# A two-layer decoder trunk on one core: two thirds of the expert weight matrices by accumulating scatters instead of one-hot products

## The chip, the core and the metric

The kernel runs on one core of one Trainium2 chip. The metric is the device time of one execution in microseconds, and less is better. The engines are named as in the profile: PE (TensorE) multiplies matrices, DVE (VectorE) and ACT (ScalarE) work element by element, POOL (GpSimd) issues here most of the transfers between memory and SBUF, every indirect one among them, and SP issues the weight loads. PEld is PE's loading of the stationary operand, which overlaps its products.

## The reference, cut to what matters

Two layers, each a mixer part and an expert part ("PEER"); the change is about the expert part alone. For 512 tokens and 16384 experts per layer:

```python
def block(xt):                       # 128 tokens of 1024 columns
    q = (xt @ w_pq).reshape(128, 8, 2, 128)
    s = einsum('thpd,hpkd->thpk', q, sub_keys)
    v1, i1 = top_k(s[:, :, 0], 16)   # per head: 16 best of 128 first keys
    v2, i2 = top_k(s[:, :, 1], 16)   # and of 128 second keys
    cand = v1[..., :, None] + v2[..., None, :]
    top, pos = top_k(cand, 16)       # the 16 best pairs of a head
    eidx = i1 * 128 + i2 at pos      # an expert is a pair of keys
    g = softmax(top)
    a = gelu(einsum('thkd,td->thk', u_tab[eidx], xt))
    return einsum('thk,thkd->td', g * a, v_tab[eidx])
```

Each token thus has 8 heads x 16 = 128 chosen experts with a weight each.

## The kernel before

**Two ways through the experts.** The tokens lie in four blocks of 128. Three blocks (`DB = 3`, 384 tokens, `SD`) go the dense way: PE computes the hidden value of every expert for every token, from 128 panels of `u_tab` (128 experts each), ACT applies gelu and writes the 128 x 384 result to memory (`h_d`, "expert_spill" in the trace). The weights of the same tokens stand in a second matrix in memory (`g_d`, "weight_spill"), of which nearly all entries are zero. In the last stage both are read back, multiplied on DVE (`wgt`) and used as stationary operand against 128 panels of `v_tab`. The fourth block goes the sparse way: 128 indirect gathers fetch one chosen row of `u_tab` for each token, 4 KB each (`urow`), and one product and sum on DVE, a "dot", follows for each; later 128 gathers of `v_tab` rows follow the same way (`vrow`).

**A panel** is a 1024 x 128 weight block. SP loads it (`raw`), ACT rounds it (`split_hi`), DVE subtracts the rounded part (`split_lo`, one pass over 128 x 1024), and PE multiplies in three passes of eight (`gemm`, L458 to L460), over 384 columns, or over 512 for the mixer and `w_pq`. ACT and DVE prepare a panel two ahead (`LEAD = 2`); four raw and four split buffers go round.

**Stages of the expert part**, in the order of every engine's program:
1. Heads: eight heads, each with 2 panels of `w_pq` and `T_U = 8` panels of `u_tab`. Beside them DVE finds the best keys and pairs of the head (`best`, `rest`, `pairs`, `pairs_at`, `pairs2`, `places`), and beside the first two panels of the next head it looks up the keys (`key_of`, three passes over 128 x 1024 for each of two sides).
2. R1: `REST = 8` panels. At their start DVE ends the last head, takes the softmax of all heads at once and writes `idu`, the rows to gather, for all 128 slots. POOL waits for that, gathers six rows (`UR = 6` buffers), and after that each row once the dot that frees its buffer is done. After the sixth panel (`SEL_AT`) PE turns the key numbers and weights round, so that the 128 slots of a token stand on the partitions.
3. G: `N_G = 48` groups of `GT = 8` tokens, a panel beside each. DVE compares the key numbers with 0 to 127 (`hot`, two passes over 128 x 1024), ACT scales the first by the weights (`scale_hot`, eight instructions), and PE multiplies the two for each token (L938): that gives the token's 128 x 128 weight matrix. ACT copies it out of PSUM to `stage`, and POOL writes `stage` to `g_d` after each four groups (32 tokens, 2 MB).
4. R2: `REST = 8` panels. V: the 128 panels of `v_tab`, with the last dots and the `v_tab` gathers beside them.

The table `DOTS` says how many dots DVE does after each panel from R1 on (two beside most panels of R1 and R2, three beside two groups of G, then 24 panels of V). Every engine runs its own program in order, so a wait on DVE for a gathered row holds back the next `split_lo`, and with it PE two panels on. POOL's program is one order as well:

```python
pool.wait_ge(idu_ready, l + 1)
for k in range(UR):
    gather_u(k)
for n in range(LATE_U):              # then along R1, G, R2
    for k in range(dots_by(n - 1) if n else 0, dots_by(n)):
        if k + UR < SLOTS:
            gather_u(k + UR)         # waits for dot k
```

Of the kernel before, what the change touches and what calls it, by code (L numbers as in the profile page):

```python
# [15 lines left out]
ACT = mybir.ActivationFunctionType  # L16
# [8 lines left out]
P = 128  # L25
# [12 lines left out]
NEG = -3.0e38  # L38
PH, TOPK, NKEYS = 8, 16, 128
# [6 lines left out]
N_G = SD // GT  # L46
# [14 lines left out]
T_U = 8  # L61
# [8 lines left out]
M_R2 = M_G + NTB * BLK_U  # L70
# [4 lines left out]
A_R2 = A_G + NTB * BLK_U  # L75
# [77 lines left out]
LATE_U = 2 * REST + NTB * BLK_U  # L153
DOTS_V = 24
DOTS = [0, 0] + [2] * (REST - 2) + [1, 2] * (N_G // 2) + [2] * (REST - 2) + [0, 0] + [1, 1, 2] * (DOTS_V // 3)

# [6 lines left out]
def dots_by(p):  # L163

    return sum(DOTS[:p + 1])
# [18 lines left out]
class Chain:  # L184
# [3 lines left out]
    def __init__(self, eng, sem, per_layer):  # L188
        self.eng, self.sem, self.per_layer = eng, sem, per_layer
        self.layer, self.base, self.n = 0, 0, 0  # L190

    def start(self, layer):
        self.layer, self.base, self.n = layer * self.per_layer, 0, 0

    def mark(self, ins):
        ins.then_inc(self.sem, 1)
        self.n += 1

    def wait(self):
        self.eng.wait_ge(self.sem, self.layer + self.base + self.n)  # L200

    def link(self, ins):
        self.mark(ins)
        self.wait()

    def enter(self, i, count):

        self.outer, self.inner, self.count = self.base, self.n, count
        self.base, self.n = i * count + (self.base + self.n), 0

    def leave(self, times):
        assert self.n == self.count, (self.n, self.count)
        self.base, self.n = self.outer, self.inner + times * self.count


DVE_CHAIN = 266


def build_trunk(nc, xT, c, pos, freq, bands, w_mod, b_mod, w_in, w_sT, b_s, qkv_gain, w_uq, w_ukv,
                w_pool, pool_scale, w_abc, w_o, w_pq, keysT, uT_tab, u_rows, v_tab, fin_gain, out, dve_chain):  # L220
# [29 lines left out]
    ones = sb("ones", [P, P])  # L250
    causal = sb("causal", [P, P])
    ident16 = sb("ident16", [P, P], BF16)
    causal16 = sb("causal16", [P, P], BF16)
    iota = sb("iota", [P, P])
    eps = sb("eps", [P, 1])
    cos = sb("cos", [P, TT, HALF])
# [56 lines left out]
    sel1T = sb("sel1T", [P, S])  # L313
    sel2T = sb("sel2T", [P, S])
    gT = sb("gT", [P, SD])
# [84 lines left out]
    g_sub, g_exp, g_norm = sem("g_sub"), sem("g_exp"), sem("g_norm")  # L400
    sel_turned, sel_act, sel_dve = sem("sel_turned"), sem("sel_act"), sem("sel_dve")
# [183 lines left out]
    def _(pool):  # L585
# [19 lines left out]
        pool.wait_ge(consts_made, 2)  # L605
        for half in range(2):
            pool.dma_start(g_d[half, 0:1, 0, :16], ones[0:1, :16]).then_inc(stage_out[half], 16)
        for l in range(DEPTH):
# [10 lines left out]
            pool.dma_start(ukv[:].rearrange("p a b -> p (a b)"), one(w_ukv)).then_inc(params_in, 16)  # L619
            for j in range(3 * KC):  # L620
# [57 lines left out]
            pool.wait_ge(idu_ready, l + 1)  # L678
            for k in range(UR):
                gather_u(k)  # L680
            for n in range(LATE_U):
                for k in range(dots_by(n - 1) if n else 0, dots_by(n)):
                    if k + UR < SLOTS:
                        gather_u(k + UR)
                b = n - REST
                if 0 <= b < NTB * BLK_U and b % BLK_U == BLK_U - 1:
# [4 lines left out]
                    if b == NTB - 1:  # L691
# [3 lines left out]
                r = n - REST - NTB * BLK_U  # L695
# [5 lines left out]
                if r == 1:  # L701
                    pool.wait_ge(stage_out[0], 16 + l * (8 * NTB) + 8 * NTB)
                    pool.wait_ge(stage_out[1], 16 + l * (8 * NTB) + 8 * NTB - 16)
# [5 lines left out]
            pool.wait_ge(stage_out[1], 16 + l * (8 * NTB) + 8 * NTB)  # L709
# [26 lines left out]
    def _(pe):  # L736
        pe.wait_ge(consts_made, 2)
        pe.wait_ge(identr_made, 1)
        with pe.Fori(0, DEPTH) as l:
# [145 lines left out]
            settle(pe)  # L885
            with pe.Fori(0, PH // 2) as two:
# [350 lines left out]
    def _(dve):  # L1237
# [55 lines left out]
        for l in range(DEPTH):  # L1293
# [254 lines left out]
            for h in range(PH):  # L1548
# [232 lines left out]
```

## Time and profile before

| | us |
|---|---|
| median of 3 runs | 3599.91 |
| lowest of them | 3599.59 |
| the profiled execution | 3599.65 |
| its span, first to last instruction | 3597.9 |
| PE busy in the span | 3484.4 (97%) |
| DVE busy | 2483.5 (69%) |
| ACT busy | 1463.0 (41%) |
| POOL busy | 879.9 (24%) |

The first layer's expert part lies from about 447 us to 1790 us after the span's start, the second's about 1775 us later with the same picture. The profile names an instruction by its line in the kernel, its engine, its operation and what it writes and reads, as `urow<-in_u_rows,idu`.

### The profile page before, as it was taken

Reading aid. Unit: us, or ns where it says so; the run is one execution under the profiler, and the core shown is the slowest. Engines: PE = TensorE matmul, PEld = TensorE weight load, DVE = VectorE, ACT = ScalarE, POOL = GpSimd, SP = SyncE. Lnnn points to the kernel's source line nnn. Section 1 sums busy time; section 2 is a strip of 40 time slices with the busy share of each in tenths; the row PEclk is TensorE's granted clock in tenths of the full one; section 3 lists DMA queues with packets and bytes.
Section 4 is the critical chain, followed back from the end, with each engine's and each line's share of the span. In section 5 each row is a group of like instructions: output and inputs, shape, how many; then the busy total and the mean of one; then the engine's idle time right before and its main releaser. Section 6 shows DMA issues by size and latency. Waiting matters only on the chain.

```text
span 3597.9 us, 53854 instructions
## 1 busy us (share of the span) xinstructions
PE 3484.4 (97%) x18220; PEld 2936.6 (82%) x18220; DVE 2483.5 (69%) x4639; ACT 1463.0 (41%) x2538; POOL 879.9 (24%) x1027
## 2 busy tenths in 40 slices
PE   5999999999999999999989998999999999999998
PEld 3776789999999777777767776999999997777775
DVE  6455688889888775555464566888898878655554
ACT  3334233335776333323243333333367753323322
POOL 0010100004334534444400010000053345344442
PEclk8999999999999999999999999999999999999999
DMA  7353434447999988999744433444499999899995
GB/s 258 116 190 125 149 122 148 146 150 287 355 342 340 395 326 338 358 350 346 290 148 153 161 127 120 149 150 150 147 339 345 342 359 379 300 357 352 357 349 199
DMA packets 269525, 909.67 MB, mean 253 GB/s; under 512 B 32212, under 2 KB 65028, under 8 KB 268452
## 3 DMA queue, kind: packets, MB, share of 16 engines
q0 software_dynamic: 126496, 473.44, 35.8%
q1 hardware_dynamic: 105984, 383.83, 29.8%
q10 hardware_dynamic: 36868, 50.35, 3.9%
q8 instruction: 74, 1.21, 0.1%
q14 instruction: 103, 0.84, 0.1%
HBM read 792.14 MB, written 115.34 MB: 252 GB/s over the span
## 4 chain that ended last, share of the span: by engine, by line
PE 92%; DVE 3%; DMA 3%; issue 1%; ACT 1%; POOL 0%; ACTq 0%; SPq 0%; DVEq 0%; POOLq 0%
PE ps L458 16%; PE ps L460 15%; PE ps L459 15%; PE ps L958 10%; PE ps L959 10%; PE ps L960 10%; PE ps L938 5%; PE ps L972 3%; PE ps L776 2%; DMA urow<-in_u_rows,idu 1%; PE ps L832 1%; DMA mod<-in_w_mod 1%; PE ps L899 1%; PE ps L873 1%; PE ps L874 1%
## 5 line engine op out<-in xcount | busy, mean ns | idle before, releaser
L458 PE MATMUL ps<-mov,whl 128*128 128x384 f32 (+1 forms) x2880 | 1042.5, 362 | 48.2 <-DVE whl L445 30.4
L460 PE MATMUL ps<-mov,whl 128*128 128x384 f32 (+1 forms) x2880 | 1014.8, 352 | 0.0
L459 PE MATMUL ps<-mov,whl 128*128 128x384 f32 (+1 forms) x2880 | 1012.2, 351 | 0.0
L445 DVE TENSOR_TENSOR whl<-raw,whl 128x1024 fp32r<-128x1024 f32 x648 | 793.3, 1224 | 205.1 <-ACT whl L435 188.1
L435 ACT CAST whl<-raw 128x1024 fp32r<-128x1024 f32 x648 | 680.0, 1050 | 107.3 <-ACT hst L1148 74.8
L958 PE MATMUL ps<-whl,wgthl 128*128 128x512 f32 x1536 | 614.3, 400 | 14.9 <-DVE wgthl L1646 14.8
L458 PEld LDWEIGHTS ps<-mov,whl 128*128 128x128 f32 x2880 | 543.0, 189 | 102.9 <-issue 38.5
L959 PE MATMUL ps<-whl,wgthl 128*128 128x512 f32 x1536 | 610.6, 398 | 0.0
L960 PE MATMUL ps<-whl,wgthl 128*128 128x512 f32 x1536 | 610.1, 397 | 0.0
L667 POOL DMA_INDIRECT urow<-in_u_rows,idu x256 | 304.5, 1189 | 1225.7 <-DVE idu L1579 787.3
L460 PEld LDWEIGHTS ps<-mov,whl 128*128 128x128 f32 x2880 | 542.3, 188 | 35.3
L459 PEld LDWEIGHTS ps<-mov,whl 128*128 128x128 f32 x2880 | 543.7, 189 | 31.4 <-issue 2.4
L1208 ACT CAST wgthl<-wgt 128x384 fp32r<-128x384 f32 x256 | 131.3, 513 | 830.6 <-PE ps L960 630.4
L1646 DVE TENSOR_TENSOR wgthl<-wgt,wgthl 128x384 fp32r<-128x384 f32 x256 | 142.8, 558 | 379.1 <-ACT wgthl L1208 332.0
L958 PEld LDWEIGHTS ps<-whl,wgthl 128*128 128x128 f32 x1536 | 290.3, 189 | 110.8 <-issue 25.2
L960 PEld LDWEIGHTS ps<-whl,wgthl 128*128 128x128 f32 x1536 | 290.4, 189 | 70.8
L959 PEld LDWEIGHTS ps<-whl,wgthl 128*128 128x128 f32 x1536 | 290.5, 189 | 69.3
L1592 DVE CUSTOM_DVE_ANT_0 urow<-urow,htok 128x1024 f32<-128x1024 f32 x256 | 306.4, 1218 | 35.2 <-DMA urow<-in_u_rows,idu 35.1
L675 POOL DMA_INDIRECT vrow<-in_v_tab,idv x256 | 264.0, 1031 | 259.5 <-PE ps L972 190.7
L1148 ACT ACTIVATE hst<-ps 128x384 f32<-128x384 f32 x256 | 123.5, 483 | 364.9 <-PE ps L460 349.6
L1175 ACT ACTIVATE hotg<-hotg,gT 128x128 f32<-128x128 f32 x768 | 234.9, 391 | 10.7 <-DVE hotg L1601 10.7
L657 POOL DMA_DIRECT2D hin<-expert_spill x256 | 144.6, 570 | 352.4 <-DVE wgt L1634 334.2
(245 smaller groups left out, 3453.9 us busy)
## 6 DMA issues: line engine op xcount, KB each, us to landing
raw<-in_uT_tab SPq DMA_DIRECT2D x256, 512.0 KB
raw<-in_v_tab SPq DMA_DIRECT2D x256, 512.0 KB
expert_spill<-hst ACTq DMA_DIRECT2D x256, 192.0 KB
hin<-expert_spill POOLq DMA_DIRECT2D x256, 192.0 KB
gt<-weight_spill POOLq DMA_DIRECT2D x64, 768.0 KB
weight_spill<-stage POOLq DMA_DIRECT2D x22, 2048.0 KB
raw<-in_w_in SPq DMA_DIRECT2D x72, 512.0 KB
raw<-in_w_mod SPq DMA_DIRECT2D x64, 512.0 KB
```

The source lines that it names most:

```text
L435: nc.scalar.copy(whl[:, m % RING, 0], raw[:, raw_n(m) % RAW]).then_inc(hi_done, 1)
L445: nc.vector.tensor_tensor(whl[:, m % RING, 1], raw[:, raw_n(m) % RAW], whl[:, m % RING, 0].bitcast(F32), ALU.subtract).then_inc(lo_done, 1)
L458: nc.tensor.matmul(o, w[:, 0, k], src[:, 0, k, :cols], start=(k == 0), stop=False)
L459: nc.tensor.matmul(o, w[:, 0, k], src[:, 1, k, :cols], start=False, stop=False)
L460: mm = nc.tensor.matmul(o, w[:, 1, k], src[:, 0, k, :cols], start=False, stop=(k == KC - 1))
L667: pool.indirect_dma_start(urow[:, k % UR], None, u_rows, bass.IndirectOffsetOnAxis(idu[:, k:k + 1], 0)).then_inc(u_in[k % UR], 16)
L675: pool.indirect_dma_start(vrow[:, slot], None, v_tab.rearrange("a p d -> (a p) d"), bass.IndirectOffsetOnAxis(idv[:, q, j:j + 1], 0)).then ...
L958: nc.tensor.matmul(o, ghi, hi, start=first, stop=False)
L959: nc.tensor.matmul(o, ghi, lo, start=False, stop=False)
L960: mm = nc.tensor.matmul(o, glo, hi, start=False, stop=last)
L1175: ins = nc.scalar.activation(one, one, ACT.Copy, scale=gT[:, e * GT + t:e * GT + t + 1])
L1592: nc.vector.tensor_tensor_reduce(urow[:, k % UR], urow[:, k % UR], htok[:], 1.0, 0.0, ALU.mult, ALU.add, act_in[:, k:k + 1]).then_inc(dot_ ...
```

## The change

Of the three dense blocks only the first keeps the one-hot products (`OHB = 1`, `OH = 128` tokens, so `N_G = 16` groups). For the other two (`N_TS = 2`, 256 tokens):
- Their part of `g_d` is filled with zeros at the start of each layer, by eight transfers of 2 MB from a zeroed tile, issued by POOL after the loads of `uq` and `ukv`.
- After each head DVE computes, for the two blocks, at which element of `g_d` each of the 16 weights of a token belongs (`chosen`, table `idg`), and POOL issues 16 x 2 = 32 indirect transfers, each of one 4-byte weight per partition, 128 in all, that add to memory (`scatter`). The 32 of a head wait until all of the head before have landed. That is 256 such transfers in a layer.
- The softmax is taken head by head (`shares`; ACT's Exp stands beside the tenth panel of a head), and the rows to gather are known head by head too. So 8 dots stand beside each head from the second to the eighth (`DOTS_H`), 56 in all, and 72 remain for R1, G, R2 and 18 panels of V. POOL puts the gathers for them behind the 27th to the 32nd scatter of each head, save the last.
- A head has `T_U = 12` panels of `u_tab` instead of 8. With 16 groups instead of 48 the sum stays: 96 + 8 + 16 + 8 = 128 panels.
- PE turns the fourth block's tokens round (`turn_rows`) in the first head and no longer after the last, and 5 tiles instead of 11 after the sixth panel of R1.
- The helper that numbers DVE's chained steps (`Chain`) is shortened to what is used.

```diff
-T_U = 8
+T_U = 12
+N_TS = 2
+OHB = DB - N_TS
+OH = OHB * P
+N_OH = OH // TB
+N_G = OH // GT
+DOTS_H = (0, 0, 0, 0, 0, 0, 0, 0, 0, 1, 1, 2, 2, 2)
+DOTS_A = sum(DOTS_H) * (PH - 1)
+DOTS_V = 18
...
+            for b in range(N_OH, NTB):
+                pool.dma_start(g_d[:, :, b].rearrange("a p x -> p a x"),
+                               zero[:].unsqueeze(1).to_broadcast([P, P // AG, P])).then_inc(zero_out, 16)
...
-            pool.wait_ge(idu_ready, l + 1)
-            for k in range(UR):
-                gather_u(k)
+            def scatter(h):
+                pool.wait_ge(idg_ready, l * PH + h + 1)
+                pool.wait_ge(g_norm, l * PH + h + 1)
+                pool.wait_ge(sc_out, l * (16 * N_TS * SLOTS) + 16 * N_TS * TOPK * h)
+                late = list(range(h * sum(DOTS_H), (h + 1) * sum(DOTS_H))) if h + 1 < PH else []
+                for n in range(N_TS * TOPK):
+                    k, t = h * TOPK + n // N_TS, n % N_TS
+                    settle(pool)
+                    pool.indirect_dma_start(g_d.rearrange("a p b (x o) -> (a p b x) o", o=1),
+                                            bass.IndirectOffsetOnAxis(idg[:, t, k:k + 1], 0),
+                                            topv[:, OHB + t].rearrange("p h k -> p (h k)")[:, k:k + 1], None,
+                                            compute_op=ALU.add).then_inc(sc_out, 16)
+                    if n >= 26 and late:
+                        gather_u(late.pop(0) + UR)
+                for k in late:
+                    gather_u(k + UR)
+            for h in range(PH):
+                pool.wait_ge(idu_ready, l * PH + h + 1)
+                if h == 0:
+                    for k in range(UR):
+                        gather_u(k)
+                scatter(h)
...
+            def shares(h):
+                dve.wait_ge(g_exp, l * PH + h + 1)
+                sums, share = den[:, h * TT:(h + 1) * TT], topv[:, :, h]
+                chain.link(nc.vector.tensor_reduce(sums, share, AX, ALU.add))
+                chain.link(nc.vector.reciprocal(dinv[:, h * TT:(h + 1) * TT], sums))
+                nc.vector.tensor_tensor(share, share, dinv[:, h * TT:(h + 1) * TT].unsqueeze(2).to_broadcast([P, TT, TOPK]),
+                                        ALU.mult).then_inc(g_norm, 1)
+
             for h in range(PH):
                 for j in range(2 + T_U):
                     split_lo(dve, l, M_T + h * (2 + T_U) + j + LEAD)
                     if j < 2 and h:
                         key_of(h - 1, j)
+                    if j == 1 and h:
+                        chosen(h - 1)
+                    if j == 10:
+                        shares(h)
+                    if h:
+                        at = (h - 1) * sum(DOTS_H)
+                        dots_between(at + sum(DOTS_H[:j]), at + sum(DOTS_H[:j + 1]))
```

Two places show it in the programs. **POOL, from the heads to G.** Before, its whole row from the load of the keys to the first write of `stage`:

```order
L648 DMA keys<-in_keysT 128x2048 [waits merged,gemm_done]
L667 DMA urow<-in_u_rows,idu 128x1024 [waits idu_ready,dot_done]
L667 DMA urow<-in_u_rows,idu 128x1024 [waits dot_done] x23
L694 DMA weight_spill<-stage 128x32x128 [waits stage_ready]
```

Now, from the gathers at the end of the seventh head's scatter on (a gather's line is L671 in the new kernel, a scatter's L691):

```order
L671 DMA urow<-in_u_rows,idu 128x1024
L691 DMA weight_spill<-topv,idg 6291456x1
L671 DMA urow<-in_u_rows,idu 128x1024 x3
L691 DMA weight_spill<-topv,idg 6291456x1 x32
L671 DMA urow<-in_u_rows,idu 128x1024 x18
L722 DMA weight_spill<-stage 128x32x128
```

The 32 scatters of the last head stand in one piece, with no gather among them, and the 18 gathers for R1 and the first groups of G stand behind them.

**DVE, at the end of the last head and the start of R1.** Before:

```order
L445 TENSOR_TENSOR whl<-raw,whl 128x1024
L1571 COPY den<-topv 128x32
L1572 TENSOR_TENSOR topv<-topv,den 128x512
L1541 TENSOR_TENSOR eq<-abf,iota 128x1024
...
L1577 SCALAR_TENSOR_TENSOR idf<-sel_106,sel_107 128x128
L1579 TENSOR_SCALAR idu<-idf,lbase 128x128
L445 TENSOR_TENSOR whl<-raw,whl 128x1024
L1582 TENSOR_REDUCE den<-topv 128x32
L1583 RECIPROCAL dinv<-den 128x32
L1584 TENSOR_TENSOR topv<-topv,dinv 128x512
```

Now:

```order
L1620 ISA urow,act_in<-urow,htok 128x1024
L1620 ISA act_in 128x1
L1581 TENSOR_TENSOR eq<-abf,iota 128x1024
...
L1601 SCALAR_TENSOR_TENSOR idf<-sel_108,sel_109 128x16
L1602 SCALAR_TENSOR_TENSOR place<-sel_109,sel_108 128x32
L1603 TENSOR_SCALAR place<-sel_108 128x32
L1604 TENSOR_SCALAR idu<-idf,lbase 128x16
L1605 TENSOR_SCALAR place<-place 128x32
L1606 SCALAR_TENSOR_TENSOR place<-place 128x32
L1611 TENSOR_SCALAR idg<-place,tokat 128x16 x2
```

The dots (`ISA urow,act_in`) stand beside the heads now, the softmax of all heads is gone from here, and behind the last `key_of` come the eight small steps of `chosen` that release the last 32 scatters.

## Rows read from the trace of the kernel before

**Rows 1.** Busy time per engine by stage, first layer: heads, R1, G, R2, V
```profile
core 0: us, PE busy (x) PEld busy (x) DVE busy (x) ACT busy (x) POOL busy (x), PEclk, DMA share, GB/s
...
459.00:831.00 372.00, 370.83 (x2058) 353.85 (x2058) 314.12 (x959) 127.96 (x166) 0.00 (x0) 1.00 0.42 146
831.00:866.00 35.00, 35.00 (x208) 34.97 (x208) 28.61 (x36) 17.29 (x25) 17.25 (x14) 1.00 0.81 306
866.00:1154.00 288.00, 287.89 (x1928) 287.61 (x1927) 253.63 (x298) 224.69 (x528) 106.98 (x87) 1.00 0.98 345
1154.00:1195.00 41.00, 32.70 (x187) 32.07 (x186) 24.65 (x34) 13.05 (x18) 21.71 (x21) 0.96 1.02 385
1195.00:1790.00 595.00, 594.88 (x2772) 445.51 (x2773) 347.03 (x512) 184.96 (x254) 262.38 (x328) 1.00 0.91 345
```
**Rows 2.** Chain that ended last, 840 to 1200 us: start, length, what
```profile
856.32 1.20 PE ps L924 x11
870.01 1.78 PE ps L938 x16
876.09 2.02 PE ps L938 x16
...
1145.13 1.78 PE ps L938 x16
1151.10 1.78 PE ps L938 x16
```
**Rows 3.** ACT's copies of the queries, first layer: count, ns, first and last start
```profile
L1161 ACT COPY qh<-ps x16: 586/587/587, 466.5 to 794.5; 128x512 f32<-128x512 f32 x16
```
**Rows 4.** Waits of DVE, 459 to 840 us: in all, times, longest
```profile
DVE whl L445 <- ACT whl L435: 31.0, 25, 4.2
DVE v L1480 <- PE ps L899: 18.0, 8, 2.4
```
**Rows 5.** Groups of POOL's instructions: count, busy us, mean ns, idle before
```profile
L667 POOL DMA_INDIRECT urow<-in_u_rows,idu x256 | 304.5, 1189 | 1225.7 <-DVE idu L1579 787.3 <-DVE act_in L1592 393.2 <-issue 44.5
L675 POOL DMA_INDIRECT vrow<-in_v_tab,idv x256 | 264.0, 1031 | 259.5 <-PE ps L972 190.7 <-issue 68.8
L657 POOL DMA_DIRECT2D hin<-expert_spill x256 | 144.6, 570 | 352.4 <-DVE wgt L1634 334.2 <-DMA expert_spill<-hst 15.3 <-issue 2.5
L694 POOL DMA_DIRECT2D weight_spill<-stage x24 | 41.9, 1748 | 1.7 <-issue 1.6
```
**Rows 6.** Timeline of POOL from 840 us: start, length, what, idle before
```profile
840.83 1.12 POOL L667 DMA_INDIRECT urow<-in_u_rows,idu  x1 [393.70 <-DVE idu L1579]
...
845.17 0.94 POOL L667 DMA_INDIRECT urow<-in_u_rows,idu  x1 [0.31 <-issue]
846.41 0.94 POOL L667 DMA_INDIRECT urow<-in_u_rows,idu  x1 [0.30 <-issue]
...
872.32 1.99 POOL L667 DMA_INDIRECT urow<-in_u_rows,idu  x1 [0.30 <-issue]
```
**Rows 7.** Timeline of DVE in R1
```profile
839.64 0.29 DVE L1579 TENSOR_SCALAR idu<-idf,lbase 128x128 uint32<-128x128 f32 x1
...
846.71 1.23 DVE L1592 CUSTOM_DVE_ANT_0 urow<-urow,htok 128x1024 f32<-128x1024 f32 x1 [2.80 <-DMA urow<-in_u_rows,idu]
847.86 0.08 DVE L1592 DVE_READ_ACCUMULATOR2_ANT act_in<- 128x1 f32 x1
...
862.04 1.22 DVE L445 TENSOR_TENSOR whl<-raw,whl 128x1024 fp32r<-128x1024 f32 x1
863.18 0.55 DVE L1611 COPY gT<-ps 128x384 f32<-128x384 f32 x1
863.76 1.22 DVE L1601 TENSOR_TENSOR hotg<-sel1T,iota 128x1024 f32<-128x1024 f32 x1
```
**Rows 8.** Timeline of ACT in R1, the first group's scaling
```profile
865.08 2.46 ACT L1175 ACTIVATE hotg<-hotg,gT 128x128 f32<-128x128 f32 x8 [1.31 <-DVE hotg L1601]
```
**Rows 9.** Timeline of PE across the idle time ahead of V
```profile
1187.05 0.34 PE L460 MATMUL ps<-mov,whl 128*128 128x384 f32 x1
1194.77 0.80 PE L958 MATMUL ps<-whl,wgthl 128*128 128x512 f32 x1 [7.38 <-DVE wgthl L1646]
```
**Rows 10.** Chain that ended last, 1130 to 1200 us: V's first products
```profile
1196.42 0.43 PE ps L958
...
1197.70 0.43 PE ps L958
...
1198.70 0.23 PE ps L958
```
**Rows 11.** Busy time per engine in the first layer's mixer
```profile
60.00:110.00 50.00, 50.00 (x212) 38.48 (x211) 30.26 (x37) 18.59 (x27) 0.00 (x0) 1.00 0.54 189
110.00:160.00 50.00, 50.00 (x217) 36.45 (x216) 24.05 (x63) 17.73 (x27) 0.00 (x0) 1.00 0.33 105
```
**Rows 12.** DMA queues of the page: packets, MB, share of 16 engines
```profile
q0 software_dynamic: 126496, 473.44, 35.8%
...
q10 hardware_dynamic: 36868, 50.35, 3.9%
```

More of the change, by code:

```diff
@@ L163, in dots_by @@
 def dots_by(p):
-    return sum(DOTS[:p + 1])
+    return DOTS_A + sum(DOTS[:p + 1])
 assert dots_by(LATE_U + DOTS_V - 1) == SLOTS
@@ L184, with __init__, link @@
 class Chain:
[L188 to L195, printed above, removed]
+    def __init__(self, eng, sem):
+        self.eng, self.sem, self.n = eng, sem, 0
+    def link(self, ins):
         ins.then_inc(self.sem, 1)
         self.n += 1
[L199 to L216, printed above, removed]
+        self.eng.wait_ge(self.sem, self.n)
 def build_trunk(nc, xT, c, pos, freq, bands, w_mod, b_mod, w_in, w_sT, b_s, qkv_gain, w_uq, w_ukv,
-                w_pool, pool_scale, w_abc, w_o, w_pq, keysT, uT_tab, u_rows, v_tab, fin_gain, out, dve_chain):
+                w_pool, pool_scale, w_abc, w_o, w_pq, keysT, uT_tab, u_rows, v_tab, fin_gain, out):
     gate_d = nc.dram_tensor("gate_spill", [3 * KC, P, S], F32, kind="Internal").ap()
@@ L883, in _, with turn_rows, two_heads @@
             sum_squares(pe, l, SQ_H2 + KC - 1, 2, False, True)
-            settle(pe)
-            with pe.Fori(0, PH // 2) as two:
+            def turn_rows():
+                for c in range(KC):
+                    o = ps[:, 4 + c // 4, c % 4 * P:(c % 4 + 1) * P]
+                    nc.tensor.matmul(o, mov[:, 0, c, SD:], identr[:], start=True, stop=False)
+                    mm = nc.tensor.matmul(o, mov[:, 1, c, SD:], identr[:], start=False, stop=True)
+                mm.then_inc(htok_turned, 1)
+            def two_heads(two, first=False):
                 for n in range(2 * (2 + T_U)):
@@ L890, in _ @@
                     gemm(pe, l, m, more=two * (2 * (2 + T_U)), more_half=two * (2 + T_U),
-                         rows=None if n else (mov_ready, l * 3 * KC + 2 * KC), cols=S if j < 2 else SD)
+                         rows=(mov_ready, l * 3 * KC + 2 * KC) if first and n == 0 else None, cols=S if j < 2 else SD)
+                    if first and n == 1:
+                        turn_rows()
                     if j in (2, 3):
@@ L903, in _ @@
                         mm.then_inc(score_ready, 1)
+            two_heads(0, first=True)
+            settle(pe)
+            with pe.Fori(1, PH // 2) as two:
+                two_heads(two)
             def experts(first_m, times):
@@ L1157, in _ @@
                     split_hi(act, l, m + LEAD)
+                    if j == 9:
+                        act.wait_ge(g_sub, l * PH + h + 1)
+                        nc.scalar.activation(topv[:, :, h], topv[:, :, h], ACT.Exp).then_inc(g_exp, 1)
+                    if h == 0 and j == 4:
+                        act.wait_ge(htok_turned, l + 1)
+                        nc.scalar.copy(htok[:], ps[:, 4:6].rearrange("p b c -> p (b c)")).then_inc(htok_ready, 1)
                     if j < 2:
@@ L1293, in _ @@
         for l in range(DEPTH):
-            chain.start(l)
             dve.wait_ge(bias_in, l * 16 + 16)
@@ L1548, in _, with dots_between @@
+            def dots_between(k0, k1):
+                for k in range(k0, k1):
+                    if k == 0:
+                        dve.wait_ge(htok_ready, l + 1)
+                    dve.wait_ge(u_in[k % UR], l * 16 * len(range(k % UR, SLOTS, UR)) + 16 * (k // UR + 1))
+                    nc.vector.tensor_tensor_reduce(urow[:, k % UR], urow[:, k % UR], htok[:], 1.0, 0.0, ALU.mult, ALU.add,
+                                                   act_in[:, k:k + 1]).then_inc(dot_done, 1)
             for h in range(PH):
```

125 lines of the change are left out of this document (66 added, 59 removed).

## The prediction

> **What bounds the kernel now.** I read the busy times by stage first, because the change shortens one stage, lengthens another and moves work between them. From the heads to V, PE is busy in all but about 10 us of 1331 us, and the rest lies in R2 [rows 1]. So what PE is spared counts in full as long as no other engine makes it wait. Next to it DVE is the fullest: 314.12 of 372 us in the heads, 253.63 of 288 in G. POOL does nothing beside the heads. Second comes the chain that ended last [rows 2]: in G it stays on PE, from the first group's products at 870.01 to the last one's at 1151.10 us, 47 steps of 5.98 us, of which 1.78 us are the products of eight tokens and 4.20 us the panel. Third, the head's period: ACT copies the queries twice a head, after each panel of `w_pq`, so the 328.0 us from the first copy to the sixteenth are seven periods and one such panel of 24 products at 0.23 us, 5.6 us: 46.1 us a head [rows 3, 10].
>
> **What PE is spared.** 32 of 48 groups go in each layer: 32 x 1.78 = 57.0 us. Of 11 tiles turned in R1, which take 1.20 us, 6 go: 0.65 us [rows 2]. The eight products that turn the fourth block only change place. Per layer 57.6 us, for both 115 us, with nothing waiting: 3597.9 - 115.2 = 3482.7 us.
>
> **The heads.** Four more panels make a head 46.1 + 4 x 4.20 = 62.9 us. Two engines must keep up.
> DVE: it had 314.12 / 8 = 39.3 us of work in a head. To that come four splits of 1.22 us, eight dots of 1.23 us, and some dozen small steps for the places and the shares, below 0.3 us each by the 128-column step in [rows 7]: 39.3 + 4.9 + 9.8 + 3 = 57 of 62.9 us. The dots stand at the tenth to the fourteenth panel, where only `places` was near, and the place arithmetic at the second, ahead of a wait of up to 2.4 us that DVE had anyway [rows 4]. So DVE alone delays nothing; without that cover it would be about 1.3 us a head. ACT's eight Exp, with a table change each way, fall in its idle 65% of the heads.
> POOL: 32 scatters and 8 gathers a head. The trace has no scatter and no transfer that adds. Its nearest rows are the gathers, also 128 separate pieces each: 0.94 to 1.99 us with 0.30 us between two [rows 6], on average 1.03 us where DVE is 58% busy (V) and 1.19 us in R1 to V, where the dots are [rows 1, 5]. With gaps: from 1.24 to 2.29 us, on average 1.33 and 1.49. In the heads DVE is 90% busy, so I take 1.49: 40 x 1.49 = 59.6 us, and about 1 us of waiting for dots, in 62.9 us. It fits with 2 us to spare. A gather that comes late behind its 27 scatters may still hold up a dot here and there: 1.5 us a layer in all, as an allowance.
> What an adding transfer costs more than a gather is the unknown of this case; below, it is the first rival.
>
> **The end of the heads: a wait takes back half.** The rows for the last dots are gathered by POOL in the same order as the scatters. When the last head ends, 56 dots are done and 62 rows gathered. R1's dots 57 to 62 have their rows; the 63rd, which stands at R1's sixth panel, has not: its gather stands behind all 32 scatters of the last head, and these wait for the last head's keys. Counted from R1's first panel on PE, at 831.0 us (870.01, less nine panels of 4.20 us, less 1.20 us) [rows 2]:
> - the last indices were there at 839.93 us, so after 8.9 us [rows 7]; with six more small steps 9.5 us;
> - 32 scatters: DVE will mostly stand still then, so 1.33 us each [rows 5, 6]: 42.6 us, so 52.1 us;
> - from the start of a gather's issue to the start of its dot 846.71 - 840.83 = 5.9 us [rows 6, 7]: 58.0 us;
> - two dots (2.3 us), split and copy (862.04 to 863.76, 1.7 us), the comparison until ACT starts (1.3 us) and its eight scalings, 2.46 us [rows 7, 8]: 65.8 us.
> Only then can PE multiply the first group. Without the wait it would be there at 39.0 - 0.65 = 38.4 us. PE stands still for 27.4 us. What is queued on DVE behind the waiting dot is the split of G's first panel, the copy of the weights, the first two comparisons; PE and ACT both wait for these. The second group is late as well: DVE has two splits, a comparison, the `v_tab` indices, four dots and the next comparison between the two, some 8.6 us, then come ACT's 2.46 us, against 6.0 us of PE's work and the 2.6 us of the first scaling: 2.6 us. And after PE stood still for 7.4 us ahead of V, its first eight products came 0.43 us apart instead of 0.23 us, the 1.2 GHz step of its clock instead of 2.4 [rows 9, 10]: 1.6 us more after such a wait. Together 31.6 us a layer. Bounds: with 1.24 us a scatter 28.7 us, with 2.29 us 62 us.
>
> **The zeros.** Eight transfers of 2 MB a layer take the place of as many that were written from `stage` in G; the bytes are the same, but they move into the mixer. POOL issues them in 8 x 1.75 us [rows 5] and next has work more than 100 us later. The engines for transfers are 54% and then 33% busy there [rows 11], and 16.8 MB at the 345 GB/s of G [rows 1] are 49 us of all of them, so they land by about 160 us, long before the first scatter. PE's weight loads share the engines with them: in G such loads ran beside 98% and PE lost 0.1 us [rows 1]. The mixer needs two loads a panel instead of one. I take 2 us a layer, between 0 and 10. In G nothing is gained by fewer writes, since PE did not wait for them.
>
> **The sum.** Per layer 57.6 - 31.6 - 1.5 - 2 = 22.5 us. Span: 3597.9 - 45 = 3553 us. The profiled execution's time is 1.8 us above its span, and the median 0.3 us above that: **3555 us**, 1.2% less. A measurement of this kernel can tell about 2% from no change, so this is no change by that bound. With the cheap ends (1.24 us, no loss in the heads or by the zeros) it is 3542 us; with 1.56 us a scatter, the most for which POOL keeps up, and 10 us for the zeros, 3586 us.
>
> **Rivals.**
> 1. *POOL becomes the bound of the heads.* It decides from 32 s + 8 x 1.49 + 1 > 62.9, so from s = 1.56 us a scatter with its gap; an adding transfer has to fetch what it adds to, and the step from 1.49 is small. For it speaks that gathers of 1.99 us occur beside dots [rows 6]; against it that the average beside an equally busy DVE is 1.19. Above it each 0.1 us costs 7 x 3.2 us in the heads and 3.2 us at the end, 51 us for both layers. Break-even with the kernel before (22.5 us a layer) is near 1.62 us, the bound of 2% slower near 1.76 us; at 1.8 us the time is about 3690 us, at 2.29 us 3940 us. Dots would wait for their rows at the last panels of each head, and PE two panels on. The Trainium skill, "SBUF — State Buffer", section "Who interferes with whom", says that a DVE instruction with two SBUF inputs contends with a GpSimd instruction that reads SBUF, and that the loser is blocked, not slowed. The spread of one and the same gather in [rows 6] agrees with that; by that rule alone scatters beside a DVE that is 90% busy would lie nearer 2.29 than 1.49 us.
> 2. *The transfer engines become the bound.* 128 pieces on 16 engines are 8 each, 256 for a head. 42% of the engines' time in the heads is taken [rows 1], so 36.5 us are left and a piece may take 143 ns. The nearest rows: ACT's queue, 36868 packets of 1.4 KB, had 3.9% of 16 x 3597.9 us, 61 ns each; POOL's queue, 126496 of 3.7 KB, 163 ns [rows 12]. Small pieces are nearer the first, which gives 16 us a head and hides. At 300 ns a head would need 132 us: some 69 us more for each of 16 heads, 4660 us. The Trainium skill, "DMA: Bandwidth & Descriptors", section "Specifications", puts the smallest transfer at full rate at 512 B and says that below it the engine reads, modifies and writes; no row here shows a write of 4 B.
> 3. *The last head's scatters are cheap.* If issuing one is like issuing a direct transfer, 0.57 us [rows 5], so 0.87 us with its gap, the wait at the end falls by 14.7 us a layer and the loss in the heads goes: 3522 us. Against it: a gather of as many pieces never took less than 0.94 us in these rows.
>
> **How the numbers follow.** Forecast (3540 to 3600 us) 0.53; rival 1 0.25, of which 0.10 stays under 3672 us; rival 2 0.10; rival 3, or a wait that is shorter for another reason, 0.12. Faster by over 2%: 0.12. Within 2%: 0.53 + 0.10 = 0.63. Slower: 0.15 + 0.10 = 0.25. A range from 3500 to 3720 us takes in the forecast, nearly all of rival 3 and 0.14 of rival 1: about 0.79.
>
> **What the profile would show.** The products of L938's successor 256 times a layer less, and G some 190 us shorter. POOL's scatters at 1.2 to 1.3 us of issue in the heads. A wait of DVE for `urow` of some 30 us at R1's sixth panel in each layer, and behind it one of PE of about 27 us ahead of G's first products, with a lower clock after it. Heads of 63 us with DVE near 90%. Wrong would make it: scatters above 1.56 us, a share of the transfer engines near 1 in the heads, or weight loads that PE waits for while the zeros are written.

## The result: 6% slower, outside the range

The changed kernel takes **3814.7 us** (median of four runs, 3812.42 to 3825.74) against 3599.75 us for the kernel before on the same chip: a ratio of 1.060, 95% interval 1.059 to 1.0615. Forecast were 3555 us and a range that ends at 3720 us. The profiled execution took 3813.35 us, its span is 3811.6 us. One of the four runs of the kernel before took 7039.04 us; why is not known, and the ratio leaves it out.

The head of the page of the changed kernel, and of its queues:

```profile
PE 3392.8 (89%) x17184; PEld 2864.5 (75%) x17184; DVE 2367.1 (62%) x4673; ACT 1300.3 (34%) x2004; POOL 1791.8 (47%) x1544
...
PE   5999898878866999999989998988888389999998
POOL 2001028888886443444311010488888845344442
...
q0 software_dynamic: 200224, 473.73, 39.0%
...
PE 57%; POOL 25%; issue 7%; DMA 5%; DVE 5%; ACT 1%; ACTq 0%; SPq 0%; POOLq 0%; DVEq 0%
```

PE has 92 us less work and waits 305 us more (3811.6 - 3392.8 against 3597.9 - 3484.4). POOL had 0% of the chain that ended last before; now it carries a quarter of it, and in the slices of the heads it is busy 8 tenths of the time. The groups on which this rests, with what the engine waited for ahead of them:

```profile
L691 POOL DMA_INDIRECT weight_spill<-topv,idg x512 | 903.7, 1765 | 156.9 <-issue 155.4 <-DMA weight_spill<-topv,idg 0.9 <-DVE act_in L1620 0.6
...
L451 PE MATMUL ps<-mov,whl 128*128 128x384 f32 x2048 | 712.9, 348 | 260.3 <-DVE whl L438 153.2 <-DVE gT L1677 107.0
```

A scatter is 1765 ns of POOL and 155.4 us / 512 = 0.30 us of gap: 2.07 us, where the forecast had 1.49 in the heads and 1.33 behind them, and where POOL could keep up only below 1.56. Only 1.5 us of the idle time ahead of 512 scatters is for anything but POOL itself.

By stage in the first layer (the columns are those of [rows 1]): the heads but for the end of the last one, the last 123 us before G's first products, G, R2, and V with the first 13 us of what follows it:

```profile
459.00:1040.00 581.00, 495.52 (x2631) 473.42 (x2632) 405.28 (x1115) 187.38 (x238) 417.36 (x252) 0.91 0.65 171
...
1063.00:1186.00 123.00, 54.48 (x291) 53.81 (x291) 45.19 (x67) 21.07 (x34) 100.73 (x66) 0.72 0.56 134
...
1186.00:1280.00 94.00, 94.00 (x636) 94.00 (x635) 83.12 (x99) 72.79 (x168) 41.73 (x32) 1.00 0.97 346
1280.00:1319.00 39.00, 31.02 (x177) 30.38 (x176) 23.91 (x34) 12.18 (x17) 19.59 (x19) 0.93 1.02 392
1319.00:1914.00 595.00, 591.19 (x2853) 451.95 (x2853) 346.27 (x510) 189.10 (x261) 250.84 (x320) 1.00 0.89 338
```

G itself is as foreseen: 94 us of PE without a gap instead of the 288 of [rows 1]. The loss is ahead of it. In the last 123 us before G, PE works 54 us at a granted clock of 0.72, and POOL 101.

ACT's copies of the queries give the head's period, as in [rows 3], and the first and last products of G and V the stages behind:

```profile
L1206 ACT COPY qh<-ps x16: 585/587/587, 472.8 to 1006.7; 128x512 f32<-128x512 f32 x16
```

(1006.7 - 472.8 - 5.6) / 7 = **75.5 us a head**; forecast were 62.9, before it was 46.1. From the last copy to G's first product it is 1186.2 - 1006.7 = 179.5 us.

The waits of PE in this last stretch (1007 to 1190 us: in all, times, longest), and of DVE:

```profile
PE ps L451 <- DVE gT L1677: 54.0, 1, 54.0
PE ps L451 <- DVE whl L438: 24.5, 2, 14.5
...
DVE urow L1620 <- DMA urow<-in_u_rows,idu: 93.9, 8, 56.1
```

The 54.0 us are the wait that the prediction named, with twice its length: a dot waits for its row, and behind it on DVE stand the split and the copy of the weights. POOL's timeline at this place shows why (start, length, what, idle before):

```profile
1103.32 1.52 POOL L671 DMA_INDIRECT urow<-in_u_rows,idu  x1 [0.30 <-issue]
1105.14 1.93 POOL L671 DMA_INDIRECT urow<-in_u_rows,idu  x1 [0.31 <-issue]
1107.38 2.64 POOL L691 DMA_INDIRECT weight_spill<-topv,idg  x1 [0.30 <-issue]
1110.33 1.97 POOL L691 DMA_INDIRECT weight_spill<-topv,idg  x1 [0.31 <-issue]
...
1123.60 1.54 POOL L691 DMA_INDIRECT weight_spill<-topv,idg  x1 [0.30 <-issue]
1125.45 1.55 POOL L691 DMA_INDIRECT weight_spill<-topv,idg  x1 [0.30 <-issue]
```

The seventh head's turn of POOL, with the gathers for the last two dots of the last head and for R1's first six, runs until 1107 us. DVE waits 14.4 us for the first of these rows, and PE two panels on, 14.5 us until 1098 us; the other 10.0 us of the second row of PE's waits are the same wait one head earlier, until 1016.7 us. Then the last head's 32 scatters begin, with R1's gathers behind them, and the 54.0 us follow. A scatter is 1.54 us at best. It is as short as that in a row where DVE stands still for the missing row (from 1119 us on), and 2 to 2.6 us at times where DVE works. In the whole first layer 81 of the 256 scatters have no DVE instruction beside them, and all of these take 1.54 to 1.58 us.

### The profile page after: what moved, and what is told of

Its sections match the earlier page's. It is cut to its first block, busy times and chain, and to the rows that moved or that the text cites. A ratio compares the mean times of both kernels' runs of the same rounds, so it can differ in the third digit from the quotient of the medians.

```text
span 3811.6 us, 51491 instructions
## 1 busy us (share of the span) xinstructions
PE 3392.8 (89%) x17184; PEld 2864.5 (75%) x17184; DVE 2367.1 (62%) x4673; ACT 1300.3 (34%) x2004; POOL 1791.8 (47%) x1544
## 3 DMA queue, kind: packets, MB, share of 16 engines
q1 hardware_dynamic: 105984, 383.83, 29.6%
## 4 chain that ended last, share of the span: by engine, by line
PE 57%; POOL 25%; issue 7%; DMA 5%; DVE 5%; ACT 1%; ACTq 0%; SPq 0%; POOLq 0%; DVEq 0%
POOL weight_spill L691 21%; PE ps L997 9%; PE ps L998 9%; PE ps L999 9%; PE ps L451 6%; PE ps L453 6%; PE ps L452 6%; POOL urow L671 3%; PE ps L1011 3%; DMA raw<-in_w_in 2%; PE ps L804 2%; DMA urow<-in_u_rows,idu 2%; PE ps L977 1%; PE ps L901 1%; PE ps L860 1%
## 5 line engine op out<-in xcount | busy, mean ns | idle before, releaser
L451 PE MATMUL ps<-mov,whl 128*128 128x384 f32 (+1 forms) x2880 | 1058.5, 368 | 306.2 <-DVE whl L438 180.5
L452 PE MATMUL ps<-mov,whl 128*128 128x384 f32 (+1 forms) x2880 | 1031.0, 358 | 0.0
L453 PE MATMUL ps<-mov,whl 128*128 128x384 f32 (+1 forms) x2880 | 1030.4, 358 | 0.0
L691 POOL DMA_INDIRECT weight_spill<-topv,idg x512 | 903.7, 1765 | 156.9 <-issue 155.4
L451 PEld LDWEIGHTS ps<-mov,whl 128*128 128x128 f32 x2880 | 558.8, 194 | 367.5 <-issue 302.2
L997 PE MATMUL ps<-whl,wgthl 128*128 128x512 f32 x1536 | 603.9, 393 | 17.3 <-DVE wgthl L1712 17.3
L998 PE MATMUL ps<-whl,wgthl 128*128 128x512 f32 x1536 | 599.8, 391 | 0.0
L999 PE MATMUL ps<-whl,wgthl 128*128 128x512 f32 x1536 | 599.5, 390 | 0.0
L453 PEld LDWEIGHTS ps<-mov,whl 128*128 128x128 f32 x2880 | 556.5, 193 | 35.4
L452 PEld LDWEIGHTS ps<-mov,whl 128*128 128x128 f32 x2880 | 558.9, 194 | 31.4 <-issue 2.3
L671 POOL DMA_INDIRECT urow<-in_u_rows,idu x256 | 310.2, 1212 | 392.2 <-DVE idu L1604 183.7
L1248 ACT CAST wgthl<-wgt 128x384 fp32r<-128x384 f32 x256 | 131.4, 513 | 799.8 <-PE ps L999 716.4
```

What stands on the lines that cost most here:

```text
L451: nc.tensor.matmul(o, w[:, 0, k], src[:, 0, k, :cols], start=(k == 0), stop=False)
L452: nc.tensor.matmul(o, w[:, 0, k], src[:, 1, k, :cols], start=False, stop=False)
L453: mm = nc.tensor.matmul(o, w[:, 1, k], src[:, 0, k, :cols], start=False, stop=(k == KC - 1))
L671: pool.indirect_dma_start(urow[:, k % UR], None, u_rows, bass.IndirectOffsetOnAxis(idu[:, k:k + 1], 0)).then_inc(u_in[k % UR], 16)
L691: pool.indirect_dma_start(g_d.rearrange("a p b (x o) -> (a p b x) o", o=1), bass.IndirectOffsetOnAxis(idg[:, t, k:k + 1], 0), topv[:, OHB ...
L997: nc.tensor.matmul(o, ghi, hi, start=first, stop=False)
```

## The experiments

Medians are device times; "before" is the kernel before, run beside the others on the same chip. e1 to e4 ran beside a before of 3601.14 us, e5 to e7 of 3601.07, e8 to e10 of 3600.57.

**e1: no scatters.** The 512 transfers are not issued, so the two blocks' weights stay zero; the indices, shares, zeros, panels and dots are all there.

```diff
-                    pool.indirect_dma_start(g_d..., IndirectOffsetOnAxis(idg[:, t, k:k + 1], 0),
-                                            topv[...][:, k:k + 1], None, compute_op=ALU.add).then_inc(sc_out, 16)
```

> The changed kernel with the 512 scatters left out (the weights of two blocks stay zero); the places, the zeros, the gathers and dots beside the heads stay. Theory A (POOL's issue of the scatters, 2.07 us each with its gap, is the bound of the heads and of the end of the last head): a head's period falls from 75.5 to about 63 us, PE's wait of 54 us ahead of G's first products goes, and the time is about 3470 us: 3483 of the bare sum, 12 more for the zeros, some 30 less because V is 15 us shorter per layer in the changed kernel. Rival B (DVE's added work, the dots and place steps, or ACT's Exp beside the heads, holds PE up): the period stays above 70 us and the time above 3650 us.

Measured: 3465.38 us (3463.2 to 3466.06), ratio 0.962 (0.9606 to 0.9635). Copies of the queries, and PE's waits over the whole span:

```profile
L1198 ACT COPY qh<-ps x16: 586/587/589, 473.7 to 919.5; 128x512 f32<-128x512 f32 x16
...
PE ps L451 <- DVE whl L438: 30.4, 6, 19.8
```

The head's period is (919.5 - 473.7 - 5.6) / 7 = 62.9 us, to the tenth what was worked out, and the wait for `gT` is gone from the list. So 349 us hang on the scatters alone. In the heads, DVE with its added work and dots and ACT's Exp delay nothing.

**e2: scatters that don't add.** One argument less: the weight overwrites what lies there. Where two heads choose the same element of a token, only the later weight is kept.

```diff
-                                            topv[...][:, k:k + 1], None, compute_op=ALU.add)
+                                            topv[...][:, k:k + 1], None)
```

> The changed kernel with each scatter as a plain write instead of an addition (where two heads of a token choose the same expert one weight is lost). If the addition is what makes the issue of a scatter cost 1.54 us at least and 1.77 us on average instead of a gather's 0.94 and 1.2: issue near 1.0 to 1.2 us, heads near 63 us, about 3530 us in all. If any scatter of 4-byte pieces costs that: no change, 3810 us. Between: 3600 to 3750 us.

Measured: 3578.04 us (3574.67 to 3580.98), ratio 0.9938 (0.9923 to 0.9953). Its group of scatters, its queue, its copies, and PE's wait for the first group's weights:

```profile
L691 POOL DMA_INDIRECT weight_spill<-topv,idg x512 | 617.5, 1206 | 199.7 <-issue 151.8 <-DVE idg L1610 47.9
...
q0 software_dynamic: 142880, 473.73, 36.4%
...
L1205 ACT COPY qh<-ps x16: 585/587/590, 474.1 to 933.6; 128x512 f32<-128x512 f32 x16
...
PE ps L451 <- DVE gT L1676: 65.3, 2, 32.8
```

A scatter that does not add is 1206 ns, and its median by itself is 958 to 972 ns: a gather's time. With its gap that is 1.51 us, almost the 1.49 of the forecast. The period falls to 64.8 us and the wait ahead of G to 32.8 us. So the direction of the transfer and its 4-byte pieces cost POOL nothing beside a gather; **the addition costs 0.56 us a scatter**, and 237 of the 349 us. The queue shows that an adding transfer is more packets: against the 126496 of [rows 12], plain scatters add 16384, which is 32 each, and adding ones 73728, which is 144 each. That POOL's time goes with this number is likely, and was not tried by itself.

The 3530 us expected for this case were missed by 48. Even at 1.51 us a scatter POOL is at work or between two issues in all but 18.5 of the 387 us from its first gather to the last copy: the period is 1.9 us above 62.9 (2.4 in the second layer), and from the last copy to G's first product it is 131.4 and 127.9 us against 89.9 in e1. The 113 us by which e2 is above e1 are the price of 512 plain scatters.

**e3: the zeros beside the heads.** e1, with one of the eight zero transfers behind each head's turn of POOL instead of all in the mixer; the first gathers for R1 follow the last of them. Scatters are left out here too.

```diff
+                if h < NTB - N_OH:
+                    pool.dma_start(g_d[:, :, N_OH + h]..., zero[:]...).then_inc(zero_out, 16)
+            pool.wait_ge(zero_out, (l + 1) * (16 * (NTB - N_OH)))
```

> As the kernel without scatters, but the eight 2 MB fills with zeros of a layer are issued beside the heads, one a head, instead of in the mixer. If the zeros cost PE 6 us a layer in the mixer through its weight loads (the first copy of the queries comes at 472.8 instead of 466.5 us): some 12 us less than without scatters alone, about 3458 us. If not: no difference beyond 3 us.

Measured: 3472.9 us (3469.54 to 3474.59), ratio 0.9641 (0.9626 to 0.9655): 7.5 us more than e1, not less. The two halves of it (copies, then waits):

```profile
L1198 ACT COPY qh<-ps x16: 586/588/590, 467.5 to 913.3; 128x512 f32<-128x512 f32 x16
...
POOL urow L668 <- DMA weight_spill<-zero: 40.7, 2, 21.3
...
PE ps L451 <- DVE gT L1669: 20.6, 2, 11.0
```

The mixer does get its time back: the first copy comes at 467.5 us instead of 473.7 (before: 466.5), in the second layer 8.4 us earlier than in e1, counted from V's end. But POOL then waits 21 us for the last piece to land, with R1's gathers queued behind that wait, and from the last copy to G's first product it is 13.7 and 11.4 us longer than in e1. The zeros cost 6 to 8 us a layer where they stand; the place tried was worse. e9 takes another.

**e4: 32 bytes.** V was 15 us a layer shorter in the changed kernel, which no part of the change explains. One V product followed another after 0.227 us instead of 0.234, at a granted clock of 1.00 in both. In the rows of before and after (start, length, PE's instruction):

```profile
1499.92 0.40 PE L959 MATMUL ps<-whl,wgthl 128*128 128x512 f32 x1
1500.16 0.39 PE L960 MATMUL ps<-whl,wgthl 128*128 128x512 f32 x1
1500.39 0.40 PE L958 MATMUL ps<-whl,wgthl 128*128 128x512 f32 x1
```

```profile
1600.33 0.39 PE L998 MATMUL ps<-whl,wgthl 128*128 128x512 f32 x1
1600.56 0.39 PE L999 MATMUL ps<-whl,wgthl 128*128 128x512 f32 x1
1600.79 0.39 PE L997 MATMUL ps<-whl,wgthl 128*128 128x512 f32 x1
```

PEld's row for the second of the three before:

```profile
1500.16 0.19 PEld L958 LDWEIGHTS ps<-whl,wgthl 128*128 128x128 f32 x1
```

What the change does alter there is where tiles lie in SBUF, since some ahead of them got smaller or larger. `wgthl` starts at byte 180960 of a partition before and at 179328 after. It is the stationary operand of V's products: PEld loads 128 of its columns for each, and the 512 columns that move are the panel's, from `whl`, which starts at 82048 in every kernel here. The expectations of e7, e8 and e10 call `wgthl` the moving tile; what they say of its place holds, the role is the other one. e4 is the kernel before with unused memory ahead of the tiles of a layer's second half.

```diff
     top_of[0] = free
+    sb("pad", [P, 8])
     hst = sb("hst", [P, 2, SD])
```

> The kernel before with 32 unused bytes per partition ahead of the expert part's tiles, so that its weight operand in V starts at a multiple of 64 bytes as in the changed kernel (before: 32 more than one). In V a product comes every 0.235 us before and every 0.227 us after the change. If the operand's place in SBUF makes that: V 15 us shorter a layer and about 3570 us. If it is anything else: 3599 us, no change.

Measured: 3592.06 us (3588.62 to 3595.69), ratio 0.9975 (0.9964 to 0.9985): a gain of 9 us where some 30 were to be explained, with a V product every 0.233 us. So being a multiple of 64 is not all.

**e5: half of the scatters.** The changed kernel without those of the third block, whose weights stay zero.

```diff
+                    if t == 0:
                         pool.indirect_dma_start(g_d..., compute_op=ALU.add).then_inc(sc_out, 16)
```

> The changed kernel with 16 of each head's 32 scatters: those of the third token block are left out (its weights stay zero, so part of the computation is missing). Theory A (the issue time on POOL bounds the heads only while it is longer than the TensorE work of a head; behind the last head it lies on the path in full): a head needs 16 x 2.07 + 12.9 = 46 us of POOL against 62.9 us of TensorE, so the heads are at 62.9 us again as without scatters, and what is left is the last head: 16 x 1.85 us, about 30 us a layer behind the kernel without scatters. 3465 + 2 x 31 = 3527 us, between 3500 and 3550; the first V products start some 31 us later than without scatters. Theory B (the cost goes with the number of scatters, 350 us for 512 of them, whoever waits): 3465 + 175 = 3640 us.

Measured: 3509.05 us (3508.06 to 3513.68), ratio 0.9749 (0.9733 to 0.9765). Theory A. Its scatters are dearer than the changed kernel's, beside a DVE that is busy 85% of the heads instead of 69%, and the heads don't notice:

```profile
L692 POOL DMA_INDIRECT weight_spill<-topv,idg x256 | 495.4, 1935 | 174.1 <-DVE idg L1612 100.3 <-issue 73.8
...
L1207 ACT COPY qh<-ps x16: 586/587/589, 474.2 to 920.0; 128x512 f32<-128x512 f32 x16
```

The period is 62.9 us again. What is left stands behind the last head: G begins 22 to 23 us a layer later than in e1, against 30 expected. The first 256 scatters thus cost 44 us and the second 256 cost 306 us. It is a bound that is crossed, not a price per transfer.

**e7 and e10: where the stationary tile lies.** The kernel before with 160 bytes, once ahead of all tiles of the second half of a layer (e7), once just ahead of `wgthl` (e10, whose edit is shown).

```diff
+    sb("pad", [P, 40])
     wgthl = sb("wgthl", [P, 2, 2, SD], F32R)
```

> The kernel before with 160 bytes a partition of unused memory ahead of the tiles of the second half of a layer, so that the V products' moving tile starts at 181120, 128 above a multiple of 256, as in the changed kernel (179328), and not 32 above a multiple of 64. Theory P (the place of the tile in memory sets the spacing of V's products): V products every 0.227 us, 3600 - 30 = 3570 us. Theory Q (the place has no part in it, or only the 9 us that 32 bytes gave): 3590 to 3600 us, spacing 0.231 to 0.235.

> The kernel before with 160 bytes of unused memory ahead of the V products' moving tile alone (181120 instead of 180960; all other tiles stay). Theory P1 (it is where this tile starts): 0.227 us a product and 3570 us as with the pad ahead of everything. Theory P2 (it is another of the tiles that the pad moved, as the ones that VectorE or the transfers write beside the products): 3600 us, 0.235.

Measured: e7 3568.43 us (3567.39 to 3570.49), ratio 0.991 (0.9894 to 0.9927); e10 3569.68 us (3567.21 to 3574.44), ratio 0.9917 (0.99 to 0.9933). One line of V's products, before and in e10 (count, busy time, mean):

```profile
L958 PE MATMUL ps<-whl,wgthl 128*128 128x512 f32 x1536 | 614.3, 400 | 14.9 <-DVE wgthl L1646 14.8
```

```profile
L959 PE MATMUL ps<-whl,wgthl 128*128 128x512 f32 x1536 | 603.5, 393 | 17.6 <-DVE wgthl L1647 17.6
```

A V product comes every 0.227 us in both. e10 moves, besides `wgthl`, only the two tiles that lie behind it, and not `wgthl` alone, as its expectation has it: `otok`, which takes V's sums when the products are done, and `e32`, a table that DVE reads. PE reads neither in these products, so the start of `wgthl` is what remains; the other two were not moved by themselves. That is 31 us of 3600 for 160 unused bytes. So the changed kernel's time contains a gain of 30 us that has nothing to do with what it changes; with the tile where it was it would be some 3845 us.

**e6, e8, e9: one block by scatters.** From e5's bound follows a version. Only the third block is scattered (16 a head), the second goes back to one-hot products (32 groups); ten panels beside a head, and six of the last head's scatters alternate with R1's gathers. e8 adds 192 unused bytes, so that `wgthl` starts 128 above a multiple of 256 (180352 instead of 180160); e9 also moves the block's four zero transfers behind the load of the keys, where POOL waited 84 us for the first indices.

```diff
-N_TS = 2
+N_TS = 1
-T_U = 12
+T_U = 10
-DOTS_H = (0, 0, 0, 0, 0, 0, 0, 0, 0, 1, 1, 2, 2, 2)
+DOTS_H = (0, 0, 0, 0, 0, 0, 0, 0, 0, 1, 1, 2)
...
-                late = ... if h + 1 < PH else []
+                late = ... if h + 1 < PH else list(range(DOTS_A, DOTS_A + 6))
...
-                    if n >= 26 and late:
+                    if late and (n >= 12 or h + 1 == PH and n >= 5 and n % 2):
```

> Only the third token block gets its weights by scatters (16 a head), the first two by one-hot products (32 groups); ten panels beside a head, four gathers a head beside the scatters, and six of the last head's scatters alternate with gathers. Theory A: POOL needs 16 x 2.07 + 4 x 1.49 + 1 = 40 us a head and the TensorE work is 54.5 us, so POOL bounds no head. Spared against before: 16 groups x 1.78 x 2 = 57 us; given back: last head's scatters, 5 to 15 us a layer. 3530 us if the V products go at the 0.235 us spacing of before, 3500 if they go at 0.227. Theory B (a scatter in a head costs the program what it costs POOL, 0.68 us each as the changed kernel has it over the one without): 3600 - 57 + 256 x 0.68 = 3717 us.

> The kernel with one block by scatters, with 192 bytes a partition of unused memory ahead of the tiles of the second half of a layer, so that the V products' moving tile starts at 180352, 128 above a multiple of 256 (it started at 180160, 192 above one, and V's products went every 0.234 us). Theory P (where the tile starts sets the spacing): 0.227 us and 3556 - 30 = 3526 us. Theory Q (what was seen belongs to the two-product order of before alone): 3556 us.

> The same with the zeroing of the one block's weights issued behind the load of the keys, where POOL then waits 84 us for the first indices, and not in the mixer, where first head's query copy came 4 to 5 us a layer later than before. Theory A (the zeroing costs the mixer its share of the transfers, and nothing where it is moved to, since its last piece lands some 20 us after its issue, ahead of the first gathers): 3526 - 9 = 3517 us. Theory B (it costs the same wherever it is, or makes the first gathers late, as it made the gathers behind the last head late when it went out piece by piece beside the heads): 3526 to 3535 us.

Measured: e6 3556.33 us (3554.49 to 3557.67), ratio 0.9875 (0.9859 to 0.9892); e8 3535.97 us (3530.51 to 3538.28), 0.9817 (0.9801 to 0.9834); e9 **3524.5 us** (3520.23 to 3529.24), 0.9788 (0.9772 to 0.9805). From e6 and e9:

```profile
L1206 ACT COPY qh<-ps x16: 586/587/588, 470.5 to 858.2; 128x512 f32<-128x512 f32 x16
...
L691 POOL DMA_INDIRECT weight_spill<-topv,idg x256 | 462.8, 1808 | 155.5 <-DVE idg L1611 81.7 <-issue 73.5 <-DVE act_in L1620 0.3
```

```profile
L1207 ACT COPY qh<-ps x16: 586/587/587, 468.2 to 855.7; 128x512 f32<-128x512 f32 x16
```

POOL bounds nothing here (54.6 us a head, as worked out; POOL waits for indices), and theory B of e6 is out by 160 us. But 3530 was not what e6's own sum gives: 3600 - 57 + 10 to 30 us is 3553 to 3573, and 3556 lies in it. From the first copy to V's first product the layers take 702.7 and 704.2 us against 728.3 and 728.6, so 50 of the 57 us arrive; the zeros take back 4 and 5. e8 gains 20 of the 30 us expected: V is 10 and 12 us shorter, not 15, and the first copy comes 4.4 us later, which nothing here explains. In e9 the copies come 6.7 and 3.4 us earlier than in e8 and the stretch behind the last head is as long as it was: theory A by the difference, 11.5 us where 9 were expected, though the 3517 us themselves, counted from e8's missed 3526, are not reached. e9 is 2.1% faster than the kernel before, which is not clear of 2% (ratio up to 0.9805), and 7.6% faster than the changed one. 20 us of this, 0.6%, are the place of a tile (e8 against e6), and the kernel before can have its own 31 us as well (e10). Against that kernel one block by scatters is worth 3569.7 - 3524.5 = 45 us, 1.3%.

## Why the prediction was wrong

The step that failed is the price in the heads: "so I take 1.49". It was the mean of gathers beside dots, put in for a transfer that adds, and the change was safe only up to 1.56. Measured are 2.07 us with the gap, 0.56 of the 0.58 us of difference being the addition (e2 against the changed kernel: 1206 and 1765 ns).

This price was not the only thing too low. e2 pays almost exactly 1.49 us, and would be at some 3608 us with `wgthl` where it was before, not at 3555; at the same place of the tile it is 8 us slower than the kernel before (e10). "It fits with 2 us to spare" was not so either, and the wait at the end costs more than it was put at.

- **What PE is spared** (115 us): right. e1 against the kernel before with its tile at the same place (e10) is 104 us, and some 118 without the 6 to 8 us a layer for the zeros.
- **The heads** (62.9 us, 1.5 us allowed a layer): right for PE, DVE and ACT (e1), wrong for POOL: already at 1.51 us a scatter the period is 64.8 and 65.3 us (e2), so the 1.56 us up to which POOL was to keep up were too high. By the prediction's own formula POOL needs 32 x 2.07 + 8 x 1.49 + 1 = 79 us a head; PE's period became 75.5 us, 7 x 12.6 = 88 us a layer more than forecast.
- **The wait behind the heads** (27.4 us of PE): the mechanism was right, down to the instruction that waits, and for PE's wait alone its size too, for a scatter without addition (32.8 us in e2, 27.4 forecast). From the last copy to G's first product, though, e2 takes 41.5 and 38.0 us more than e1, where 31.6 were forecast. With the addition it is 54.0 us, and a part was left out: once POOL is the bound, the rows for the last two dots of a head are late too, 10.0 and 14.5 us of PE behind the last copy. From the last copy to G's first product it is 179.5 us against 89.9 in e1, so 90 us where 31.6 were forecast. A lower clock follows the wait as forecast: PE's products come 0.32 us apart instead of 0.17 for 4.4 us.
- **The zeros** (2 us a layer): 6 to 8 us, inside the bounds of 0 to 10. The engines for transfers, at 54% there before, were full, and PE worked 45 of 50 us:

```profile
60.00:110.00 50.00, 45.20 (x181) 33.94 (x180) 27.05 (x28) 16.78 (x24) 5.05 (x3) 0.97 1.00 361
```

- **V**: taken as untouched, and 15 us a layer shorter (e7, e10).
- **The sum again**, with what was measured: 3555 + 2 x (88 - 1.5 + 90 - 31.6 + 5 - 15) = 3825 us, against 3814.7.
- **Rival 1** happened, for the reason that it gave: an adding transfer costs more to issue. It had a chance of 0.25, and with its 3690 us for 1.8 us and its 51 us for each 0.1 us it gives 3828 us for 2.07. The fetch of what is added to, which it named, no run shows by itself; the runs show POOL's issue longer, with 144 packets instead of 32. DVE's part in it is the smaller one: 1.54 us is the floor where DVE stands still, and 1.84 with the gap is above 1.56 already. In the first layer all 71 scatters that take over 1.93 us have a split, a dot or another step of DVE with two tile inputs beside them, and only 86 of the 181 within 5% of the floor have. The spread from 1.54 to 2.6 us agrees with the rule of the Trainium skill ("SBUF — State Buffer", section "Who interferes with whom") that rival 1 cites. What rival 1 made of it, "nearer 2.29 than 1.49 us", is not what plain scatters took beside a DVE that was 83% busy from the first gather to the last copy: 1.51 us (e2). No run here changes DVE's work alone.
- **Rival 2** did not happen: 65% of the transfer engines' time is taken in the heads. Its 132 us a head let the share of the other transfers grow with the head; as these are a fixed 26 us (42% of 62.9), its own 300 ns give 26 + 77 = 103 us. **Rival 3** is out: a scatter never took less than a gather.

The range failed with the price. The bounds given were 1.24 to 2.29 us, so 2.07 lay inside them, yet the range was cut at 3720 us, which is 1.86 us, on the strength of a mean of another instruction.

## What to carry to other kernels

Suppose a change puts hundreds of an instruction that no row shows on one engine, and the plan holds only while it is at most 5% dearer than the nearest row. Then the forecast hangs on that threshold, and the price has to be measured alone first: here a transfer that adds cost POOL 0.56 us more than one that copies. With half of the scatters the work was free in the heads (e5); with all of them, every 0.1 us of their price cost about 42 us between e2 and the changed kernel (237 us for 0.56). So such work is to be dosed until the engine has room in the stage, as POOL had a quarter in e5 and e6, and its last portion, which nothing covers, is to be mixed with what waits behind it. And when a stage that no edit touches changes its time, look at where its operands lie before explaining it by the edit.

## What the runs showed of the hardware

- POOL issues an indirect transfer of 128 pieces of 4 bytes in 0.95 us at best, about as a gather of whole rows (0.93); one that adds takes 1.54 us at best and 144 packets instead of 32.
- A 128x512 product with a stationary tile that starts 128 above a multiple of 256 bytes came every 0.227 us (starts 179328, 181120, 180352), with one at a multiple of 256 (180992) or 192 above one (180160) every 0.233, and with one 224 above (180960) every 0.234. The moving operand began at 82048, 128 above a multiple of 256, in all of them, and no run moved it. Why is open: neither PE's loading of the tile nor ACT's and DVE's writes to it were tried alone. A rule from six places is a guess.
- Eight writes of 2 MB in the mixer took the transfer engines from 54% to 100% for 50 us; POOL's own fourth and seventh issue of them began only after 29.6 and 28.2 us of standing still, and the kernel lost 6 to 8 us a layer.
